# One-hot rows compared from PSUM, smaller gate steps in layer 0, fp16 one-hots in layer 1: a two-layer diffusion block on one core

## What is computed

```python
def peer_ffn(h, wq, k1, k2, u, v):          # 8 heads, 128 keys a side, top 16, 16384 experts
    q = (ht @ wq).reshape(n_tok, PEER_HEADS, PEER_QDIM)
    s1 = jnp.einsum('thd,kd->thk', q[..., :PEER_HALF], k1)
    s2 = jnp.einsum('thd,kd->thk', q[..., PEER_HALF:], k2)
    t1, i1 = lax.top_k(s1, PEER_TOPK)
    t2, i2 = lax.top_k(s2, PEER_TOPK)
    # the best 16 of the 16*16 sums; idx = i1 * 128 + i2; g = softmax of the 16 sums
    ...
    act = jax.nn.gelu(jnp.einsum('td,thkd->thk', hb, ue), approximate=False)
    return jnp.einsum('thk,thkd->td', gb * act, ve)
```

## Time and profile before

| | us |
|---|---|
| median of 3 runs | 5429.59 |
| lowest and highest | 5426.74, 5431.28 |
| profiled execution, its own time | 5424.05 |
| its span, first to last instruction | 5422.3 |
| PE busy | 4579.7 (84%) |
| DVE busy | 3673.8 (68%) |
| POOL busy | 1831.0 (34%) |
| ACT busy | 1468.3 (27%) |

### The profile page before, as it was taken

The page is one execution under the profiler, slowest core; times in us unless marked ns, Lnnn a source line. Parts: engine busy times, 40 slices in busy tenths (PEclk is TensorE's granted clock), DMA queues, the critical chain, the costliest instruction groups (busy, mean ns, idle before and its releaser), DMA issues. The chain is left out here.

```text
span 5422.3 us, 76669 instructions
## 1 busy us (share of the span) xinstructions
PE 4579.7 (84%) x24359; PEld 2373.7 (44%) x24359; DVE 3673.8 (68%) x10347; ACT 1468.3 (27%) x1798; POOL 1831.0 (34%) x956
## 2 busy tenths in 40 slices
PE   8687755698999999789999974777899899899996
PEld 1244534365555555434444432434455445344442
DVE  0213334506988988889899976962787896388886
ACT  0002222003333333322222212640333333323231
POOL 0120000242222222255655545405323333445453
PEclk9797867899999999999999996888999999999998
DMA  8200000123445435577787861122344554665553
GB/s 361 90 32 14 7 1 1 71 90 128 132 141 178 149 126 177 180 305 307 309 322 310 311 238 38 48 82 75 129 147 149 186 163 139 223 214 193 213 193 117
DMA packets 416203, 852.22 MB, mean 157 GB/s; under 512 B 30468, under 2 KB 199236, under 8 KB 411844
## 3 DMA queue, kind: packets, MB, share of 16 engines
q1 hardware_dynamic: 170792, 539.25, 27.9%
q10 hardware_dynamic: 208416, 177.30, 10.3%
q0 software_dynamic: 36864, 134.23, 6.3%
HBM read 686.99 MB, written 163.68 MB: 157 GB/s over the span
## 5 line engine op out<-in xcount | busy, mean ns | idle before, releaser
L1207 POOL TENSOR_TENSOR ca_ul<-ca_ur,ca_uh 128x1024 f16<-128x1024 f32 x256 | 546.9, 2136 | 1371.4 <-ACT ca_uh L1249 1371.4
L1218 PE MATMUL ca_A<-hh,ca_uh 128*128 128x512 f16 (+1 forms) x3072 | 851.2, 332 | 120.8 <-POOL ca_ul L1207 120.8
L1218 PE MATMUL ca_A<-hl,ca_uh 128*128 128x512 f16 (+1 forms) x3072 | 849.5, 331 | 0.0
L1218 PE MATMUL ca_A<-hh,ca_ul 128*128 128x512 f16 (+1 forms) x3072 | 847.4, 331 | 0.0
L1659 PE MATMUL ex_R<-ex_vh,ex_wh 128*128 128x512 f16 x1280 | 492.7, 385 | 93.1 <-DVE ACC L1700 48.9
L1659 PE MATMUL ex_R<-ex_vl,ex_wh 128*128 128x512 f16 x1280 | 491.4, 384 | 0.0
L1659 PE MATMUL ex_R<-ex_vh,ex_wl 128*128 128x512 f16 x1280 | 491.1, 384 | 0.0
L1461 POOL TENSOR_TENSOR ex_vl<-ex_vr,ex_vh 128x1024 f16<-128x1024 f32 x128 | 323.1, 2550 | 342.7 <-ACT ex_vh L1470 342.7
L1395 DVE TENSOR_SCALAR ca_hot<-ca_iota,ca_cur 128x128 f16<-128x128 f16 (+1 forms) x1152 | 422.2, 367 | 5.1
L1218 PEld LDWEIGHTS ca_A<-hh,ca_uh 128*128 128x128 f16 x3072 | 262.0, 100 | 369.7 <-issue 77.7
L1396 DVE TENSOR_SCALAR ca_hot<-ca_iota,ca_cur 128x128 f16<-128x128 f16 (+1 forms) x1152 | 420.4, 365 | 0.0
(11 more groups left out here) (335 smaller groups left out, 7930.4 us busy)
## 6 DMA issues: line engine op xcount, KB each, us to landing
ca_ur<-in_peer_u SPq DMA_DIRECT2D x256, 512.0 KB, 3.4
ex_vr<-in_peer_v SPq DMA_DIRECT2D x256, 512.0 KB, 6.6
gates<-ca_stage ACTq DMA_DIRECT2D x36, 2048.0 KB, 10.6
mod_w<-in_mod_w SPq DMA_DIRECT2D x12, 4096.0 KB, 12.4
acts<-ca_ga ACTq DMA_DIRECT2D x128, 320.0 KB, 2.2
ex_gr<-gates SPq DMA_DIRECT2D x128, 320.0 KB, 15.5
ex_ar<-acts SPq DMA_DIRECT2D x128, 320.0 KB, 17.2
acts<-ca_ga ACTq DMA_DIRECT2D x128, 256.0 KB, 2.8
```

Source lines behind the costliest of these rows:

```text
L1207: nc.gpsimd.tensor_tensor(ul[j][:, :, :], ur[j][:, :, :], uh[j][:, :, :], ALU.subtract).then_inc(u_cut, 1)
L1218: last = nc.tensor.matmul(A[b][:, a:a + w], lhs[b][:, k, :], rhs[:, k, a:a + w], start=(k == 0 and x == 0), stop=(k == KD - 1 and x == 2))
```

## The change

The row of numbers that is compared stands in PSUM as fp32, in both layers, and no longer in SBUF (fp16 in layer 0 and on L1351, fp32 on L1395 and L1396 in layer 1). So that a PSUM bank is free for it, layer 0 has gate steps of 4 tokens instead of 8 (`E` = 16 steps a turn, `G` one bank for each buffer), and in layer 1, where `NT` is 512, `A` is 512 columns wide instead of 1024. Layer 1 is called with `full` false: fp16 one-hots in two parts, so 3 DVE instructions and 2 matmuls for each token, as in layer 0. In layer 1, 14 chunks stand ahead of a tile's gate steps instead of 12 (8 in the first half, 6 in the second), and 8 in the tail instead of 16.

```diff
-    B = 8
+    B = 8 if NT <= 512 else 4
...
-    ahead, beside = {6: (8, 6), 5: (12, 6), 4: (12, 8), 3: (20, 10)}[nt]
+    ahead, beside = {6: (8, 6), 5: (12, 6), 4: (14, 8), 3: (20, 10)}[nt]
...
+    pairs = (ahead // 2 - ahead // 4, ahead // 4)
...
-        iota = sb("iota", [P, P], F16)
...
-        A = [c.enter_context(nc.psum_tensor(f"ca_A{b}{layer}", [P, 1024], F32)) for b in range(2)]
+        A = [c.enter_context(nc.psum_tensor(f"ca_A{b}{layer}", [P, 512 if NT <= 512 else 1024], F32)) for b in range(2)]
         G = [c.enter_context(nc.psum_tensor(f"ca_G{j}{layer}", [P, B, P], F32)) for j in range(2)]
         T = G[0][:, 0:3, :]
+        row_ps = c.enter_context(nc.psum_tensor(f"ca_row{layer}", [P, P], F32))
+        row = row_ps[:, :]
...
-                        with eng.Fori(0, ahead // 4) as k:
+                        with eng.Fori(0, pairs[half]) as k:
                             for j in range(2):
-                                chunk(n * (CT // 2) + k + half * (ahead // 4), j)
+                                chunk(n * (CT // 2) + k + half * pairs[0], j)
...
-                                step.mark(nc.vector.scalar_tensor_tensor(match[:, k, :], iota[:, 0:CAND], posf[:, h, k:k + 1], ci[:, h, :],
+                                step.mark(nc.vector.scalar_tensor_tensor(match[:, k, :], row[:, 0:CAND], posf[:, h, k:k + 1], ci[:, h, :],
...
-                    gstep(nc.vector.tensor_copy(iota[:, :], iota32[:, :]))
+                    gstep(nc.vector.tensor_copy(row, iota32[:, :]))
...
-                                    row = iota32 if full else iota
-                                    nc.vector.tensor_scalar(hot[j][:, x, 0, :], row[:, :], w(0), None, ALU.is_equal)
-                                    last = nc.vector.tensor_scalar(hot[j][:, x, 1, :], row[:, :], w(1), w(2), ALU.is_equal, ALU.mult)
+                                    nc.vector.tensor_scalar(hot[j][:, x, 0, :], row, w(0), None, ALU.is_equal)
+                                    last = nc.vector.tensor_scalar(hot[j][:, x, 1, :], row, w(1), w(2), ALU.is_equal, ALU.mult)
                                     if not full:
-                                        last = nc.vector.tensor_scalar(hot[j][:, x, 2, :], row[:, :], w(1), w(3), ALU.is_equal, ALU.mult)
+                                        last = nc.vector.tensor_scalar(hot[j][:, x, 2, :], row, w(1), w(3), ALU.is_equal, ALU.mult)
...
-        peer(nc, io, mods, dram, H, HS, hh, hl, ident, 1, CTX_TILES, False, True, out=out)
+        peer(nc, io, mods, dram, H, HS, hh, hl, ident, 1, CTX_TILES, False, False, out=out)
```

More of the change, by code:

```diff
@@ L1103, in choose_and_activate @@
     PARTS = 4
-    assert tail >= 2 * PARTS and tail % 2 == ahead % 4 == beside % 2 == 0
+    pairs = (ahead // 2 - ahead // 4, ahead // 4)
+    assert tail >= 2 * PARTS and tail % 2 == ahead % 2 == beside % 2 == 0
     with ExitStack() as c:
```

## The result

The changed kernel takes 5643.99 us in the median of 4 runs (5641.93 to 5646.58) against 5429.18: a ratio of 1.0396, interval 1.0378 to 1.0414. It is slower by 215 us where 138 were forecast. By the profiled executions the span grows from 5422.3 to 5644.8 us, and the stages say where: from the first chunk to the first gather of the next stage layer 0 takes 192 us more, and layer 1 23.5 us more from its first to its last chunk; the 7 us left lie outside both.

The account below looks back on a forecast made before the run. DVE paces layer 0's gate phases, PE layer 1's and the ahead phases. 86 + 30 - 7 + 27 + 2 = 138 us on 5424.05 gives 5562, as median 5568 us, 2.5% slower; range 5500 to 5660.

Parts of the forecast that it names:

- The working's own bounds: Whole kernel: +108 us without the column copy's stall, 153 with all of it, 30 more if phases start PE at lower clock.
- the clock rival: Gate phases: PE's clock falls; at 0.75 layer 1 gains 8 us a tile, layer 0 some 4; +52, 5620; chance 0.11.
- The hold ends: One-hots and choice comparisons: a row in PSUM ends POOL's stall of DVE, some 24 and 32 us a gate phase.
- The price of a token: One-hots, both layers: 0.91 us a token from PSUM at one element a cycle, against 0.61 in layer 0, 0.45 in layer 1.
- the cheaper token (0.71 us): Rival, one-hots of both layers: the PSUM stream is not slower, two elements a cycle; sum -29 us, 5401; chance 0.11.
- the dearer one (1.09): Rival, one-hots of both layers: a PSUM operand has a fixed price; +315 us, 5745; chance 0.04.
- Layer 1: Layer 1 gate phases: DVE takes over the pace, 122.2 us against 115.4, +27 for 4 tiles; last store of gates +2.
- The split: Layer 1: two more chunks ahead in each of 4 tiles (+41), eight fewer in the tail (-41): zero.
- Layer 0, gate phase: Layer 0 gate phases: 32 steps of 3.85 us, 125.0 us a phase, +86 for 5 tiles; column copy's new stall +30.
- the signs: Gate phases if right: tokens 0.91 us, no instance over 1 us, phases near 130 and 122 us, DVE over 95% busy.
- The small steps "hidden": Layer 0 gate phase, steps of 4: PE's 92.6 us and ACT's 32 evictions for 16 (some 3 us more) are hidden.
- The sixth choice: Layer 0's last choice, over the tail: it ends the stage, and its comparisons without stall bring -7 us.

Follow-up runs that it names:

- e9: The changed kernel with the layer 1 split undone (12 chunks ahead, 16 in the tail): 5641.84 us, ratio 1.0395.
- e3: The changed kernel with four one-hot buffers of 4 tokens in layer 0 instead of two: 5579.11 us, ratio 1.0278.
- e1: The kernel before with gate steps of 4 tokens in layer 0, the row still in SBUF: 5509.81 us, ratio 1.0152.
- e5: The changed kernel with four one-hot buffers in layer 0 and the column copy in the row's PSUM bank: 5560.4 us, ratio 1.0245.
- e7: The kernel before with 8 chunks ahead and 8 beside each turn in layer 0 instead of 12 and 6: 5382.0 us, ratio 0.9914.
- e8: The changed kernel with steps of 8, fp16 row in SBUF in both layers, split 8 and 8 (layer 0), 10 and 10 (layer 1): 5344.78 us, ratio 0.9851.
- e2: The changed kernel with the column copy going to the row's PSUM bank and the pointers read from there: 5643.31 us, ratio 1.0392.

## Why the prediction was right, and what it mis-sized

The direction held, and so did the mechanism of the hold and of the slower stream. The size did not: 215 against 138 us. That it lies inside the range is in part luck. The working's own bounds, 153 us and 30 more for PE's lower level, end near 5613 us, and the measured 5644 is beyond them; the range reached to 5660 only through the clock rival and 40 us on top of it, which stand for no term of the sum.

- *The hold ends.* Right: no held one-hot in 3456.
- *The price of a token.* Right. 0.91 us was worked out from copies and casts; the three durations came out at 345, 403 and 404 ns, where the same reckoning (158 + 133 ns, and 60 for each pointer, the second of which comes with a multiplication) gives 351, 411 and 411. In layer 1, where nothing else is at work, the phase was forecast at 122.2 us and took 121.9 in the mean. So the cheaper token (0.71 us) and the dearer one (1.09) fall. The Trainium skill (VectorE: DVE Perf Modes, "The TRN2 errata") gives 120 fixed cycles from PSUM against 58 from SBUF, by estimate 65 ns an instruction. The traces do not show them either: with them the first of the three would have taken some 416 ns.
- *Layer 1.* 27 + 2 us forecast, 23.5 measured from first to last chunk. The split was called zero, and e9 shows it.
- *Layer 0, gate phase.* This is the term that was mis-sized: 125.0 us and 6 for the copy, where 146.3 were measured, 15 us a tile or 77 in all. The working adds up as 1.8 + 32 x 3.85 = 125, 12.6 for held copies, 9.8 for DVE's wait on PE: 147. The copy was priced at 6 of its 12.6 us. The wait was priced at nothing, because the count was made with PE at its high clock throughout; I had seen the low-clock chunk behind a wait and allowed 4 us a tile for it in the bounds, but not that a chunk of 9.4 us outlasts two buffers of 7.7. e3 shows it by giving DVE the run-ahead: the wait goes to zero and 65 us come back. The clock rival named this mechanism, at 4 us a tile in layer 0; it was a part of the main case and not a case of its own. Its other half did not come: in layer 1 the clock stayed at 0.97 to 0.99. (By its own terms that half would be 9.5 us a tile and not 8.) Of the signs, DVE over 95% busy came in layer 1 (121.7 of 122.9 us) and not in layer 0 (135.9 of 147.1).
- *The small steps "hidden".* Wrong as a statement on its own: e1 prices them at 80 us in the kernel before. In the changed kernel they cost through the run-ahead that they halve (65 us, e3) and through the held copy; with both mended (e5) the phase is 127 us, 2 above the stream's 125.
- *The sixth choice*, -7 forecast: from the last product to the first gather of the next stage it is 61.9 us instead of 66.7, so -5.

## What to carry to other kernels

An operand moved to PSUM frees a DVE instruction from POOL, but only instructions that stream one element a cycle anyway (two tensor operands) get that for nothing (281 ns against 279 unheld, L1353 and L1351); for a scalar comparison in fp16 it costs four times the stream, here 0.30 us a token against 0.19 of hold in layer 0 (24 us over 128 tokens). When DVE paces a phase, first move PE's free work into it: the split alone brought 47 us (e7), and with fp16 one-hots and a like split in layer 1 85 us (e8). And count buffers in us of run-ahead against the longest thing the other engine does at its lower clock, since a smaller step halves them without a line of the diff saying so.

## What the runs showed of the hardware beyond this

Two edits that each remove a real, visible stall were worth 3.0 and 12.9 us a gate phase of layer 0 alone and 19.5 together (e2, e3, e5): a part of the hold on one engine and of the wait for the other was the same time seen twice. Reading the pointers as well from PSUM made the one-hots a few ns longer (403 to 413 ns for the two with two pointers) and a layer 1 phase 2.4 us longer.

And the column copy, never held in 144 instances before, was held in the changed kernel for up to 2054 ns. The start times tell why: of its 80 instances in layer 0 before, none began while POOL made a low part; of the 160 in the changed kernel 60 did, and 59 of them were held. It is not the number of copies, for in e1, with as many of them and the row in SBUF, only one began so, and it was held (2105 ns), while 59 one-hots were. The one-hots used to meet POOL first; since they pass, the copy does.
